# A two-layer network on one core: the first stage's modulation and projections reordered by column halves

## The reference

```python
mod = silu(c) @ ada_w + ada_b              # c: 1024; ada_w: 1024 x 6144
sh1, sc1, g1, sh2, sc2, g2 = split(mod, 6)
h = rmsnorm(x, norm_mix_w) * (1 + sc1) + sh1
proj = h @ w_in                            # 1024 x 3624, split into:
# hq hf hi hg (a gated recurrence), sq sk sv (attention), iq ik iw (indexer), cu (convolution)
score[t, s] = sum_h iw[t, h] * relu(iq[t, h] . ik[s])      # 8 heads; causal; top 128 keys of each token
```

## Time and profile before

| | us |
|---|---|
| median of 3 runs (1285.32 to 1287.27) | 1285.67 |
| the profiled execution | 1284.26 |
| its span | 1282.6 |
| PE busy | 1249.5 (97%) |
| DVE busy | 850.5 (66%) |
| ACT busy | 585.3 (46%) |

### The profile page before, as it was taken

How to read it: one execution, slowest core, us unless ns; L and a number is a source line. 1 busy time by engine, 2 the same in 40 slices (tenths; PEclk the granted TensorE clock), 3 DMA queues, 4 the chain that set the end, 5 groups by cost and what they waited for, 6 DMA issues and landing times.

```text
span 1282.6 us, 18787 instructions
## 1 busy us (share of the span) xinstructions
PE 1249.5 (97%) x6603; PEld 1018.8 (79%) x6603; DVE 850.5 (66%) x1275; ACT 585.3 (46%) x840; POOL 109.2 (9%) x149
## 2 busy tenths in 40 slices
PE   4999999999999999999999999999999999999997
PEld 3777778788788888888888888888888887777786
DVE  5889987858666322444444897665466668988863
ACT  4565536443444211443333655333233347888632
POOL 9124220000000000000000000110010000000000
PEclk9999999999999999999999999999999999999999
DMA  9677952417355333333332222333232242332131
GB/s 349 188 200 147 193 127 83 131 38 226 116 164 163 99 98 93 88 98 99 98 98 83 82 82 85 96 98 115 82 98 82 83 123 58 111 109 75 50 98 66
DMA packets 209084, 146.63 MB, mean 114 GB/s; under 512 B 7490, under 2 KB 191985, under 8 KB 209024
## 3 DMA queue, kind: packets, MB, share of 16 engines
q1 hardware_dynamic: 200672, 134.40, 34.7%
q0 software_dynamic: 6128, 10.38, 4.5%
q10 hardware_dynamic: 2224, 1.05, 0.3%
HBM read 135.06 MB, written 2.10 MB: 107 GB/s over the span
## 4 chain that ended last, share of the span: by engine, by line
PE 77%; DVE 11%; ACT 6%; issue 3%; DMA 1%; POOL 1%; DVEq 0%; SPq 0%; ACTq 0%; POOLq 0%
PE banks L404 23%; PE banks L406 23%; PE banks L405 23%; ACT w_hi L376 2%; DVE w_lo L388 1%; DVE xc L2441 1%; DMA x_tok<-in_x 1%; PE banks L708 1%; POOL e L2653 1%; DVE vh L2341 1%; PE banks L625 1%; PE banks L572 1%; PE banks L1089 1%; DVE sqb L1874 1%; DVE prob L2010 1%
## 5 line engine op out<-in xcount | busy, mean ns | idle before, releaser
L388 DVE TENSOR_TENSOR w_lo<-raw,w_hi 128x1024 fp32r<-128x1024 f32 x204 | 251.0, 1235 | 122.2 <-ACT w_hi L376 116.9
L404 PE MATMUL banks<-h_hi,w_hi 128*128 128x512 f32 x792 | 318.7, 402 | 1.8 <-DVE h_lo L1865 0.9
L406 PE MATMUL banks<-h_hi,w_lo 128*128 128x512 f32 x792 | 309.6, 391 | 0.0
L405 PE MATMUL banks<-h_lo,w_hi 128*128 128x512 f32 x792 | 309.5, 391 | 0.0
L376 ACT ACTIVATE w_hi<-raw 128x1024 fp32r<-128x1024 f32 x204 | 213.5, 1051 | 173.3 <-PE banks L406 142.4
L404 PEld LDWEIGHTS banks<-h_hi,w_hi 128*128 128x128 f32 x792 | 149.2, 188 | 41.9 <-issue 8.1
L405 PEld LDWEIGHTS banks<-h_lo,w_hi 128*128 128x128 f32 x792 | 149.2, 188 | 33.4 <-issue 3.8
L406 PEld LDWEIGHTS banks<-h_hi,w_lo 128*128 128x128 f32 x792 | 149.2, 188 | 31.6
L404 PE MATMUL banks<-n_hi,w_hi 128*128 128x512 f32 x288 | 113.6, 395 | 0.9 <-DVE e L2403 0.9
L405 PE MATMUL banks<-n_lo,w_hi 128*128 128x512 f32 x288 | 112.3, 390 | 0.0
L406 PE MATMUL banks<-n_hi,w_lo 128*128 128x512 f32 x288 | 112.2, 390 | 0.0
(11 more groups left out here) (400 smaller groups left out, 1852.9 us busy)
## 6 DMA issues: line engine op xcount, KB each, us to landing
raw<-in_mlp_w SPq DMA_DIRECT2D x64, 512.0 KB, 3.8
raw<-in_a_w_in SPq DMA_DIRECT2D x48, 512.0 KB, 3.7
raw<-in_w_in SPq DMA_DIRECT2D x28, 512.0 KB, 4.4
raw<-in_ada_w SPq DMA_DIRECT2D x26, 512.0 KB, 4.5
raw<-in_b_w_in SPq DMA_DIRECT2D x24, 512.0 KB, 3.6
raw<-in_a_w_out SPq DMA_DIRECT2D x16, 512.0 KB, 3.4
raw<-in_b_w_out SPq DMA_DIRECT2D x16, 384.0 KB, 3.0
raw<-in_w_out SPq DMA_DIRECT2D x8, 512.0 KB, 4.1
```

The costliest lines, as they stand in the source:

```text
L388: dve.tensor_tensor(dst, src, hi, ALU.subtract).then_inc(split_lo, 1)
L404: pe.matmul(dst, l_hi, r_hi, start=first, stop=False)
L405: pe.matmul(dst, l_hi, r_lo, start=False, stop=False)
L406: return pe.matmul(dst, l_lo, r_hi, start=False, stop=last)
```

## The change

- c is loaded as eight rows of 128 and transposed on PE. POOL loads only the first ten parameter groups, ACT's queue the other nine; PE transposes them and ACT copies them before it squares x.
- The modulation rows for sc1 and sh1 are loaded and summed in two column halves (512 columns each, 16 tiles a half). The first half serves channel tiles 0 to 3 of h, the second tiles 4 to 7.
- The indexer's queries and the convolution's inputs and gates become "half" units: 256 output columns over four channel tiles, in two PSUM banks. PE begins units 0, 1 and 2 and the first half of the index unit (now unit 3) on channel tiles 0 to 3; DVE then sums the second half of the rows, and PE goes on with tiles 4 to 7 (units 3 to 6).
- Scores follow units 5 to 10 in place of 3 to 8. The slots of top-k rounds, conv products and taps move with them. Modulation tiles for g1 move to slots 5 to 9.

```diff
 W_IN_UNITS = (
-    [("fm", C_IQ), ("fm", C_IQ + P), ("ikw", C_IK)]
-    + [("fm", C_CU + P * m + CV * s) for m in range(CVT) for s in range(2)]
+    [("half", C_IQ, 0), ("half", C_CU, 0), ("half", C_CU + CV, 0), ("ikw", C_IK)]
+    + [("half", C_IQ, 1), ("half", C_CU, 1), ("half", C_CU + CV, 1)]
...
-ADA_AT = {0: (16, 17), 1: (18,), 2: (19,), 3: (20, 21), 4: (22,), 5: (23,), 23: (24,), 24: (25,), 25: (26, 27),
+ADA_AT = {5: (16, 17, 18), 6: (19, 20), 7: (21,), 8: (22,), 9: (23,), 23: (24,), 24: (25,), 25: (26, 27),
...
+FRONT = ([("rows", q) for q in range(4)] + ["x"] + [("rows", 4), ("rows", 5), ("w", 0), ("rows", 6), ("rows", 7), ("w", 1)]
+         + [("rows", q) for q in (8, 9, 10)] + [("w", 2)] + [("rows", q) for q in (11, 12, 13)] + [("w", 3)]
+         + [("rows", 14), ("rows", 15), ("w", 4)])
...
-ROUNDS_AT = {6: [(1,)] * 3, 7: [(1,)] * 3, 8: [(1, 2)], 9: [(1, 2)], 10: [(1, 2, 3)], 11: [(1, 2, 3)], 12: [(1, 2, 3)],
-             13: [(1, 2, 3)], 14: [(1, 2, 3)], 15: [(1, 2, 3)], 16: [(1, 2)], 17: [(1, 2)], 18: [(2, 3)], 19: [(2, 3)],
+ROUNDS_AT = {8: [(1,)] * 3, 9: [(1,)] * 3, 10: [(1, 2), (1,)], 11: [(1, 2), (1, 2)], 12: [(1, 2, 3)], 13: [(1, 2, 3), (2,)],
+             14: [(1, 2, 3)], 15: [(1, 2, 3)], 16: [(1, 2, 3)], 17: [(1, 2, 3)], 18: [(2, 3)], 19: [(2, 3)],
...
-PRODUCTS_AT = {5: 2, 6: 3, 7: 3, 8: 2, 9: 2, 10: 2, 11: 2, 12: 2, 13: 2, 14: 2, 15: 2, 16: 2, 17: 3, 18: 3, 19: 3}
-THIRDS_AT = {6: 3, 7: 3, 8: 2, 9: 2}
-PE_TAPS_AT = {9: 1, 10: 1, 11: 1, 12: 1, 13: 2, 14: 2, 15: 2, 16: 2, 17: 1, 18: 1, 19: 1}
+PRODUCTS_AT = {7: 3, 8: 3, 9: 3, 10: 3, 11: 3, 12: 3, 13: 2, 14: 2, 15: 2, 16: 2, 17: 3, 18: 3, 19: 3}
+THIRDS_AT = {8: 3, 9: 3, 10: 2, 11: 2}
+PE_TAPS_AT = {11: 1, 12: 2, 13: 2, 14: 2, 15: 2, 16: 2, 17: 2, 18: 1, 19: 1}
...
+            def row_item(q):
+                if q >= 4:
+                    sp.wait_ge(ada_dve, 2 * (q - 4) + 2)
+                if q == ROW_PAIRS // 2:
+                    sp.wait_ge(root_made, 1)
...
+            def half_step(u, k, first, last):
+                kind = W_IN_UNITS[u]
+                for n, bank in enumerate(HALF_BANKS[kind[1]]):
+                    cols = slice(n * P, (n + 1) * P)
+                    ins = three(pe, banks[:, bank, :], unit(w_hi, u, 256)[:, k % 4, cols], unit(w_lo, u, 256)[:, k % 4, cols],
+                                h_hi[:, k, :], h_lo[:, k, :], first, last)
...
+            def first_halves():
+                for u in range(3):
+                    pe.wait_ge(split_lo, u + 1)
+                    for k in range(KT // 2):
+                        if u == 0:
+                            pe.wait_ge(h_ready, H_MIX + k + 1)
+                        last = half_step(u, k, k == 0, False)
+                    last.then_inc(w_used, 1)
+                summed_columns(acc_sc1, 3 * KT, 7, range(KT // 2, KT))
+                pe.wait_ge(split_lo, U_IKW + 1)
+                for k in range(KT // 2):
+                    index_step(k)
+                pe.wait_ge(mod_ready, 3)
+                summed_columns(acc_sh1, 4 * KT, 7, range(KT // 2, KT), KT)
...
+            mixer_rows(0, (3, 0), {})
+            lo_unit(dve, 1)
+            for n in range(2 * KT, 4 * KT):
+                ada_rows(n)
+                if n == 2 * KT + 3:
+                    lo_unit(dve, 2)
+                if n == 3 * KT + 3:
+                    lo_unit(dve, U_IKW)
+                if n == 3 * KT + 5:
+                    first_scale(2, 7, KT // 2, KT)
+            lo_unit(dve, U_IQ)
+            mixer_rows(KT // 2, (7, KT), {KT - 2: U_IQ + 1})
```

More of the change, by code:

```diff
@@ L474, in _, with ring_item @@
             w_in = a["w_in"][0]
[L475 to L478, removed]
+            def ring_item(item):
+                d = arrival[item]
                 if d >= RING:
@@ L515, in _ @@
                 sp.dma_start(dst, src).then_inc(raw_in[d % RING], 16)
+            def row_item(q):
[3 more added lines that the diff above has]
+                    sp.wait_ge(root_made, 1)
+                half, g, kt = q // 8, (1, 0)[q // 4 % 2], 2 * (q % 4)
+                c = g * D + HALF * half
+                src = a["ada_w"][0, kt * P:(kt + 2) * P, c:c + HALF].rearrange("(r p) n -> p r n", p=P)
+                sp.dma_start(row_pair(q), src).then_inc(side_in[q % 4], 16)
+            for item in FRONT:
+                if item == "x":
+                    for t in range(TT):
+                        sp.dma_start(x_tok[:, t, :], a["x"][0, t * P:(t + 1) * P, :]).then_inc(x_in, 16)
+                elif item[0] == "rows":
+                    row_item(item[1])
+                else:
+                    ring_item(item)
+            for item in STREAM[U_IQ + 1:]:
+                ring_item(item)
             def stream(base, count, source, gate_tiles=False):
@@ L656, in in_unit @@
                                      h_hi[:, k, :], h_lo[:, k, :], k == 0, k == KT - 1)
+                elif kind[0] == "half":
+                    for k in range(KT // 2, KT):
+                        last = half_step(u, k, False, k == KT - 1)
                 elif kind[0] == "tm2":
@@ L1251, in shifted @@
                 for k in range(KT):
-                    if n0 == 0 and k == 1:
-                        for u in range(1, LEAD):
+                    if n0 == 0 and k == KT // 2:
+                        hi_unit(act, 1)
+                        act.wait_ge(lb_zero, 1)
+                        act.activation(lbt[:, 1, :], lbt[:, 0, :], ACT.Exp).then_inc(lb_exp, 1)
+                        for u in (2, U_IKW, U_IQ):
                             hi_unit(act, u)
-                    if n0 == 0 and k == FIRST_J:
-                        act.wait_ge(mod_ready, 3)
+                        act.wait_ge(mod_ready, 4)
+                    if n0 == 0 and k == KT - 2:
+                        hi_unit(act, U_IQ + 1)
                     act.wait_ge(h_scaled, n0 + k + 1)
@@ L1281, in read_out @@
                     return
+                if kind[0] == "half" and kind[2] == 0:
+                    return
                 act.wait_ge(w_used, u + 1)
+                if kind[0] == "half":
+                    for m, bank in enumerate(HALF_BANKS[c]):
+                        out_ = banks[:, bank, :]
+                        if c == C_IQ:
+                            ins = act.activation(iqT[:, m, :], out_, ACT.Copy)
+                        elif c == C_CU:
+                            ins = act.activation(hpad[:, m, TAPS - 1:], out_, ACT.Copy)
+                        else:
+                            ins = act.activation(cacc[:, m, :], out_, ACT.Sigmoid)
+                        ins.then_inc(evac, 1)
+                    return
+                if kind[0] == "ikw":
+                    act.activation(ikT[0:3 * IDX_D, :], banks[0:3 * IDX_D, IKW_BANK, :], ACT.Copy)
+                    act.activation(ikT[3 * IDX_D:, :], banks[0:IDX_D, IKW_BANK, :], ACT.Copy)
+                    act.activation(iwT, banks[3 * IDX_D:, IKW_BANK, :], ACT.Copy,
+                                   scale=float(IDX_HEADS * IDX_D) ** -0.5).then_inc(evac, 1)
+                    return
                 if kind[0] == "tm4":
@@ L2549, in _ @@
             chain = Chain(pool, s_pool)
+            chain.step(pool.memset(par_rows[:, :, :], 0.0))
             chain.step(pool.memset(ident[:, :], 0.0))
```

361 lines of the change are left out of this document (192 added, 169 removed).

## The result

The changed kernel takes 1298.82 us (median of 4 runs, 1298.55 to 1299.75) where the kernel before took 1285.6 in the same comparison: ratio 1.0105, 95% interval 1.0092 to 1.0118, so 13.2 us slower. The forecast was 1291.7, with a range up to 1297, and the result lies above that range. Its direction was right, its size (6.0 us) was off by a factor of two. The profiled execution has a span of 1296.7 (before 1282.6).

What follows compares the result with a forecast made beforehand. TensorE and VectorE meet at the recurrence's first level, so a gain ahead of it counts only if both win it. 5.6 + 0.8 - 0.4 = +6.0 on 1284.26, plus 1.4 to the median: 1291.7; range 1281 to 1297.

Steps and rivals of the forecast that it cites:

- c near 7: Start: c, loaded as eight rows and turned on PE, is ready at about 7.2, 5.6 earlier.
- Root 20.6, bounds 18.5 and 22: Start, ACT: parameter loads landing by about 16 hold copy and squares, so the root moves from 19.98 to 20.6.
- First product 30.0: Start, PE: first product 3.5 after DVE starts on h, at 30.0 in place of 37.9.
- T0: Time at which DVE starts on h, forecast at 26.5 with bounds 24.4 and 28.
- PE's rest of 2.9 near 50: Middle: PE waits 2.9 us for row 4 of h, ready at 53.4.
- Clock: Rival, chance 0.13: PE's 2.9 and 10 us waits each bring a half-rate spell, up to +3.2, 1293.5 to 1295.
- Slot 8 = unit 7 + 11.8: DVE's split in slot 8 follows unit 7's start: unit 7 at 75.5, slot 8 at 87.3.
- 62.5 us from slot 8 to the last decay: DVE's work from slot 8 to the last decay, 64.4 before; the decay ends at 149.8, +5.6 us.
- ACT's read-out waits some 15 us, PE some 10: ACT's hf read-out waits some 15 us for the score sums, so PE waits about 10 before conv taps.
- PE has one tap more left, +0.8; 0.4 absorbed later: Around the first level: one more conv tap on PE adds 0.8; later DVE waits absorb 0.4.
- Seen alone this is 7.9 us won: Start: the gain at PE's first product, 30.0 in place of 37.9.
- PE is 4.5 ahead: Middle, at unit 7: starts at 75.5 instead of 81.8, less 1.8 us for two score groups not yet done.

Runs made afterwards that it cites:

- experiment 5: Changed kernel with ScalarE's copy of the parameters placed behind the squares and the root instead of ahead of them: 1296.29 us, ratio 1.0079.
- experiment 6: Changed kernel with parameter copy behind the root, two busy matmuls instead of four ahead of the shift columns, TensorE's two front rests filled: 1293.01 us.
- experiment 4: Changed kernel with TensorE kept busy by three extra matmuls in each of its two rests in the front: 1295.85 us, ratio 1.0079.
- experiment 2: Changed kernel with 13 top-k block rounds of slots 8 to 15 left out altogether, so fewer keys are selected: 1292.85 us, ratio 1.0055.
- experiment 3: Changed kernel with ScalarE's conv-tap diagonals for slots 12 and 13 made ahead of the hf read-out: 1296.68 us, ratio 1.0079.
- experiment 1: Changed kernel with 13 top-k block rounds of slots 8 to 15 moved behind slot 17: 1304.5 us, ratio 1.0137.

## Why the forecast was right in sign and wrong in size

By its own steps:

- **c near 7:** 3.45. The price from the like transfer (5.4) was too high: in the changed kernel c was turned at 2.78. It changed nothing, as the tiles then waited for their bytes (1.84, and 4.57 at the ninth): eight tiles had run by 15.1, not ten.
- **Root 20.6, bounds 18.5 and 22:** 21.59. The step's term "holds the copy and the squares behind it" was mis-sized: the parameters were there at 15.64, as forecast, but behind them stand the transposes on PE (0.87) and the copy, so the squares begin at 17.00 where in experiment 5 they begin at 15.12. The root ends 1.6 us after the 19.98 of before, not 0.6. Undoing it gave 2.5 us of time, part of it clock.
- **First product 30.0:** 32.82. T0 was 27.49 (26.5); the rest is the four busy matmuls, 3.70 us in a row ahead of the shift columns, for which VectorE waits 1.83. I had read them in the code and put them at nothing. Without two of them and with the root early it is 30.15.
- **PE's rest of 2.9 near 50:** 3.15, but ending at 58.65 instead of 53.4. With the front repaired it still ends at 55.8, 2.4 late: the second sweep's 16 tiles are 0.83 apiece, not 0.785 (0.7 us in all), and four waits between them add 2.3.
- **Clock:** a rival at 0.13 and up to +3.2, from waits of 2.9 and 10 us. The mechanism was as told, but it was likelier than I gave it and one rest more brought a spell. My sum had it at nothing. From row 4 of h to unit 7 it was 24.9 us where I had 22.1 and where experiment 6, at the full level, has 22.2: 2.7 us for the spell of 57.55 to 64.37. The two spells in the front are worth 3.0 us (experiment 4). The third, at the taps, lies beside VectorE's backlog; no run takes it away alone.
- **Slot 8 = unit 7 + 11.8:** 11.8, in all three kernels looked at. The 8.0 us by which slot 8 was late (95.30 for 87.3) are exactly unit 7's 8.0 (83.53 for 75.5).
- **62.5 us from slot 8 to the last decay:** 60.6. The overcharge of 1.9 hid part of the error. It is the meetings with POOL, for which I took no change: before, four DVE rows of this stretch took 3.82 for 2.78, 2.80 for 1.22, 3.63 for 1.53 and 2.20 for 1.21, 5.7 us more in all (I counted 4.7 and missed the last), now two are, the split of slot 8 (3.24) and the score multiply (1.78 for 0.47), by 3.3.
- **ACT's read-out waits some 15 us, PE some 10:** 10.9 and 8.5.
- **PE has one tap more left, +0.8; 0.4 absorbed later:** the level started 1.8 after the decay, and the tail grew by 0.7 instead of shrinking.

The step that failed is the front and the middle up to unit 7. "Seen alone this is 7.9 us won" was 5.1 at the first product. "PE is 4.5 ahead" at unit 7 was 3.5 behind: it starts at 83.53, 1.7 after the 81.84 of before, with the same 1.8 us of score groups taken off. The terms that were wrong are the root (1.6 for 0.6), the busy matmuls (1.8 for nothing), the second sweep of tiles and the clock (2.7 for nothing in the sum). Against the forecast the kernel is 1.0 us late at T0, 2.8 at the first product, 5.3 at row 4 of h, 8.0 at unit 7 and at slot 8, 6.1 at the last decay and 7.1 at the end. Of these 7.1 us, 5.8 go when three front terms (copy, busy matmuls, rests) are undone. That the repaired kernel then lands within 1.3 us of the forecast is in part luck: its slot 8 is still 2.4 late, and the overcharge behind slot 8 pays 1.8 of it back. What I decided on, that VectorE's start in slot 8 and the score sums set the level and that TensorE's gain is not kept, held in the main: removing VectorE's work moved level and end together (experiment 2, with a share of clock), and the 5.85 us given to TensorE at the taps moved the level by 2.5 (experiment 3). That slot 8 is late because the scores begin two units later was argued and not tested: no run moves the scores.

The Trainium skill (TensorE: Matmul & The Clock Gate, Part 1) has an idle PE fall back to half rate; the spells here came after rests of 2.80, 3.15 and 8.54 us, and the first two went when their rests were filled, so the trace agrees. It agrees on what precedes a fall, not that each rest brings one: the 2.80 us of experiment 1 and the 3.39 of experiment 2 had none behind them.

## What to carry to other kernels

Here a gain at the head of the kernel was worth only what the next engine in line could take over: before moving work earlier, follow the second engine's queue to the point where both meet and price its order there. A rest of TensorE cost its length and, most times, the lower clock behind it, so the filler matmuls paid in a rest (experiment 4), and cost where they stood ahead of columns that VectorE waited for. Before a difference of 1 to 3 us is put down to an edit, compare where the lower-clock stretches lie in both traces. Work moved off a busy stretch is won only if it is tested at its new place: leaving it out altogether tells the two apart.

## What was not expected of the hardware

- A rest of 2.80 us was followed by a spell of 3.4 us at the lower level, one of 3.15 and one of 8.54 us each by a spell of 6.8 us, which had begun before the rest was over. It is not fixed: in experiment 1 the same 2.80 us rest had no spell behind it, and one stood earlier, at 26.0 to 29.4, behind a rest of 2.25; in experiments 4, 5 and 6 the rest at the taps (8.53, 8.54, 8.81) came with a spell of 10.2. In such a spell the products start every 0.427 us instead of 0.227, and one of a conv tap's two matmuls takes 1.06 us instead of 0.59.
- 4 KB of c as eight rows were in place by 2.8 us, issued at 0.9, where the same bytes one element per descriptor took 11.4, and the like eight-row transfers on POOL's queue 5.3.
- A dependent 512-column tile takes 0.83 us in both sweeps, against 0.785 in a row of conv taps.
- Beside each other, 21 executions of the kernel before spread from 1282.7 to 1288.5 us, 12 of the version with x behind the third pair only from 1282.4 to 1283.5.
